# A hybrid decoder step: two sigmoids and one PSUM read of the second LRU group moved ahead in their engines' programs

## The chip, the cores and the metric

One core of a Trainium2 chip runs the whole kernel. The metric is the device time of one execution in microseconds, as the median of several runs. Engines are called by their short names in the profile: PE is TensorE's matmul, PEld its weight load, DVE is VectorE, ACT is ScalarE, POOL is GpSimd, SP is SyncE.

## The reference, cut to what matters

One inference step of a two-layer decoder over 512 prompt tokens and 8 sample tokens, 520 columns in all, in float32. Each layer adds a retention branch and an LRU branch, merged by sigmoid gates, and then a SwiGLU. The change lies in the LRU branch:

```python
def rg_lru(xc, w_a, b_a, w_x, b_x, lam, h0):
    r = sigmoid(einsum('blnc,ncd->blnd', xb, w_a) + b_a)
    i = sigmoid(einsum('blnc,ncd->blnd', xb, w_x) + b_x)
    log_a = -LRU_C * r * softplus(-lam)
    a = exp(log_a)
    u = sqrt(-expm1(2.0 * log_a)) * (i * xf)
    _, h = associative_scan(comb, (a, u), axis=1)
xc, new_buf = causal_conv(x_lru, conv_buf, conv_w, conv_b)
hl, h_last = rg_lru(xc, ...)
lru_branch = (gelu(y_lru) * hl) @ w_lru_out
```

The convolution has four taps. The LRU's width is 1280, that is ten tiles of 128 channels.

## The kernel before

Activations lie transposed, channels on the 128 partitions and the 520 tokens along them, in two halves of 260. Every product in float32 is made of three matmuls of split operands (high by high, low by high, high by low), so each operand is kept as a high part and a low part. The weights come as a stream: SP loads a unit of up to eight 128x128 blocks into one of two buffers, POOL writes its high part (L356, a scaling copy) and its low part (L358, a subtraction) in two halves, four blocks and the rest, and PE multiplies (`product`, L370). POOL may overwrite half a buffer once PE has gone on from it (semaphore w_used).

Each engine has its own program, written out in order, and the engines meet by semaphores alone. An engine that waits holds up all that stands behind it in its program.

In the LRU stage the ten tiles are two groups of five, (g, t). A tile goes through these steps:

- PE makes the projected x. DVE reads it (`read_x`, L1115). ACT applies the first tap with the bias (`first_tap`, L1537 to L1539), DVE the three others (`conv`, L1123 and three times L1126), ACT writes the high part (`conv_high`, L1546), DVE the low part (`conv_low`, L1135).
- PE makes three results for (g, t): the two gates from the convolved x, and the projected y (`gates`). ACT reads the two gates through the sigmoid (`gate_sigmoids`, L1557 and L1560); DVE reads y (`read_y`, L1162).
- ACT goes on with two exponentials, tanh, gelu and a square root (`gate_decay`, L1566 to L1574). DVE multiplies the second gate (`gate_input`, L1169), forms a factor once tanh is there (`one_less_a2`, L1175), scans (`scan`, L1182 to L1189), and both write the split result (`gated_high`, L1551 and L1552; `gated_low`, L1194).
- In group 1, PE puts between the tiles the output products of group 0 (`lru_out`), which DVE reads (`read_out`, L1201).

PE's results of the stage go through a ring of four PSUM slots, and result n can start only when result n-4 has been read (`ring_begin`, `freed`). The results around the change are these positions of the ring's count:

- 23, 24, 25: first gate, second gate and y of (1,0), read by the two sigmoids and by read_y(1,0)
- 26, 27: output products 0 and 1 of group 0, read by read_out(0) and read_out(1)
- 28, 29, 30: the gates and y of (1,1)
- 31: output product 2; 32, 33, 34: the gates and y of (1,2)

A gate of (1,0) has two blocks, of (1,1) three; a y has eight, an output product five. So 27 waits for the read of 23, 28 for that of 24, 29 for that of 25, 30 for that of 26, and 34 for that of 30, read_y(1,1).

PE makes in this part, in order: gates(0,4), x of (1,2), x of (1,3), x of (1,4), gates(1,0), output products 0 and 1, gates(1,1), and so on. PE's program is the same before and after.

The table of ScalarE's functions is loaded by an instruction of its own (ACT_TABLE_LOAD, put in ahead of the first function that needs another table).

Of the kernel before, what the change touches and what calls it, by code (L numbers as in the profile page):

```python
# [133 lines left out]
def build(nc, wstream, xt, params, norms, tables, dec, kdt, slru, sconv, sret, ident,  # L134
          yt, ret_p, ret_s, lru_o, conv_p, conv_s, vscr):
    ctx = ExitStack()
    with ctx:
# [131 lines left out]
        def halves(ap):  # L269

            return ap.rearrange("p (t b) -> p t b", t=2)
# [6 lines left out]
        def ring(n):  # L278

            return PP[:, n % RING, :, 0:HALF] if n % RING < 2 else (  # L280
                AUX[:, 2 * (n % RING) - 4:2 * (n % RING) - 2, 0:HALF])
# [495 lines left out]
        def _(dve):  # L777
# [40 lines left out]
            with dve.Fori(0, DEPTH) as layer:  # L818
# [284 lines left out]
                def r_done(n, more=0):  # L1103
                    dve.wait_ge(s["r_done"], layer * R_TILES + (n + 1) + more)
# [13 lines left out]
                def conv(g, t):  # L1118

                    c = g * GT + t  # L1120
                    xr = XR[:, c % 2, :]
                    dve.wait_ge(s["tap_full"], layer * LT + (c + 1))
                    tt(XCF[:, t, SEQ:TOK], XCF[:, t, SEQ:TOK], SCS[:, c, :], ALU.add)  # L1123
                    for j in range(CW - 1):
                        d = CW - 1 - j
                        m = stt(XCF[:, t, d:SEQ], xr[:, 0:SEQ - d], CUR[:, PC_CW + c * CW + j:PC_CW + c * CW + j + 1],  # L1126
                                XCF[:, t, d:SEQ], ALU.mult, ALU.add)
                        if j < CW - 2:
                            dve.drain()  # L1129
                    m.then_inc(s["xc_full"], 1)  # L1130

                def conv_low(g, t):
                    dve.drain()
                    dve.wait_ge(s["xc_high"], layer * LT + (g * GT + t + 1))
                    tt(XCL[:, t, :], XCF[:, t, :], XCH[:, t, :].bitcast(F32), ALU.subtract  # L1135
                       ).then_inc(s["xc_low"], 1)
# [21 lines left out]
                def read_y(g, t):  # L1158
                    n = LRU_TILE["y", g, t] + 2
                    dve.drain()  # L1160
                    r_done(n)
                    tt(halves(YF[:, t % 2, :]), ring(n), halves(RINV[:]), ALU.mult  # L1162
                       ).then_inc(r_free[n % RING], 1)

                def gate_input(g, t):

                    b, n = t % 2, LRU_TILE["y", g, t]
                    dve.wait_ge(*freed(layer, n + 1))
                    tt(IX[:, b, :], IX[:, b, :], XCF[:, t, :], ALU.mult)  # L1169

                def one_less_a2(g, t):

                    b, c = t % 2, g * GT + t
                    dve.wait_ge(s["th_full"], layer * LT + (c + 1))
                    stt(DF[:, b, :], DF[:, b, :], 1.0, LA[:, b, :], ALU.add, ALU.mult).then_inc(s["d_full"], 1)  # L1175

                def scan(g, t):

                    b, c = t % 2, g * GT + t
                    tt(HF[:, SEQ:TOK], AF[:, b, SEQ:TOK], SLR[:, c, :], ALU.mult)  # L1180
                    dve.wait_ge(s["w_sqrt"], layer * LT + (c + 1))
                    tt(IX[:, b, :], IX[:, b, :], DF[:, b, :], ALU.mult)  # L1182
                    dve.drain()
                    dve.tensor_tensor_scan(HF[:, 0:SEQ], AF[:, b, 0:SEQ], IX[:, b, 0:SEQ], 0.0,  # L1184
                                           ALU.mult, ALU.add)
                    tt(HF[:, SEQ:TOK], HF[:, SEQ:TOK], IX[:, b, SEQ:TOK], ALU.add)
                    dve.drain()  # L1187
                    dve.wait_ge(s["y_gelu"], layer * LT + (c + 1))
                    tt(YF[:, b, :], YF[:, b, :], HF, ALU.mult).then_inc(s["gl_full"], 1)  # L1189

                def gated_low(g, t):
                    dve.drain()
                    dve.wait_ge(s["gl_high"], layer * LT + (g * GT + t + 1))
                    tt(GL[g][1][:, t, :], YF[:, t % 2, :], GL[g][0][:, t, :].bitcast(F32), ALU.subtract  # L1194
                       ).then_inc(s["gl_low"], 1)

                def read_out(m_):

                    n = LRU_TILE["o", 0, m_]
                    r_done(n)  # L1200
                    ts(halves(ACCL[:, m_, :]), ring(n), 1.0, None, ALU.mult).then_inc(r_free[n % RING], 1)  # L1201
# [16 lines left out]
                    gated_low(0, t)  # L1218
                conv_low(*FILL_X[GT - 1])
                conv(1, 3)  # L1220
                conv_low(1, 3)
                conv(1, 4)
                for t in range(GT):
                    if t == 0:
                        conv_low(1, 4)
                    else:
                        gated_low(1, t - 1)
                    gate_input(1, t)
                    read_y(1, t)
                    one_less_a2(1, t)  # L1230
                    for m_ in FILL_O[t]:
                        read_out(m_)
                    scan(1, t)
# [93 lines left out]
        def _(act):  # L1327
# [45 lines left out]
            with act.Fori(0, DEPTH) as layer:  # L1373
# [155 lines left out]
                def r_done(n, more=0):  # L1529
                    act.wait_ge(s["r_done"], layer * R_TILES + (n + 1) + more)  # L1530

                def first_tap(g, t):

                    c = g * GT + t
                    xr = XR[:, c % 2, :]
                    act.wait_ge(s["xr_full"], layer * LT + (c + 1))
                    A(CVP[:, c, :], xr[:, SEQ - CW + 1:SEQ], copy)  # L1537
                    A(CVS[:, c, CW - 2, :], xr[:, SEQ:TOK], copy)
                    A(XCF[:, t, :], xr, ACT.Identity, bias=CUR[:, PC_CB + c:PC_CB + c + 1],  # L1539
                      scale=CUR[:, PC_CW + c * CW + CW - 1:PC_CW + c * CW + CW]).then_inc(s["tap_full"], 1)  # L1540

                def conv_high(g, t):
                    if g:
                        r_done(LRU_TILE["y", 0, min(t + 1, GT - 1)] + 1)
                    act.wait_ge(s["xc_full"], layer * LT + (g * GT + t + 1))
                    A(XCH[:, t, :], XCF[:, t, :], copy).then_inc(s["xc_high"], 1)  # L1546

                def gated_high(g, t):
                    c = g * GT + t
                    act.wait_ge(s["gl_full"], layer * LT + (c + 1))  # L1550
                    A(LRO[:, c, :], HF[:, SEQ - 1:TOK], copy)  # L1551
                    A(GL[g][0][:, t, :], YF[:, t % 2, :], copy).then_inc(s["gl_high"], 1)  # L1552

                def gate_sigmoids(g, t):
                    b, c, n = t % 2, g * GT + t, LRU_TILE["y", g, t]
                    r_done(n)
                    A(halves(LA[:, b, :]), ring(n), ACT.Sigmoid,  # L1557
                      bias=CUR[:, PC_BA + c:PC_BA + c + 1]).then_inc(r_free[(n) % RING], 1)
                    r_done(n + 1)
                    A(halves(IX[:, b, :]), ring(n + 1), ACT.Sigmoid,  # L1560
                      bias=CUR[:, PC_BX + c:PC_BX + c + 1]).then_inc(r_free[(n + 1) % RING], 1)

                def gate_decay(g, t):
                    b, c, n = t % 2, g * GT + t, LRU_TILE["y", g, t]
                    act.drain()
                    A(AF[:, b, :], LA[:, b, :], ACT.Exp, scale=LAM[:, 4, c:c + 1])  # L1566
                    A(DF[:, b, :], LA[:, b, :], ACT.Exp, scale=LAM[:, 5, c:c + 1])
                    act.drain()
                    A(LA[:, b, :], LA[:, b, :], ACT.Tanh, scale=CUR[:, PC_SP + c:PC_SP + c + 1]
                      ).then_inc(s["th_full"], 1)  # L1570
                    act.wait_ge(*freed(layer, n + 2))
                    A(YF[:, b, :], YF[:, b, :], ACT.Gelu_apprx_tanh).then_inc(s["y_gelu"], 1)
                    act.wait_ge(s["d_full"], layer * LT + (c + 1))
                    A(DF[:, b, :], DF[:, b, :], ACT.Sqrt).then_inc(s["w_sqrt"], 1)  # L1574
# [6 lines left out]
                for t in range(GT):  # L1581
                    gate_sigmoids(0, t)
                    conv_high(*((0, 2) if t == 0 else FILL_X[t - 1]))
                    gate_decay(0, t)
                    first_tap(*FILL_X[t])
                    gated_high(0, t)
                conv_high(*FILL_X[GT - 1])
                first_tap(1, 3)
                conv_high(1, 3)
                first_tap(1, 4)  # L1590
                for t in range(GT):
                    gate_sigmoids(1, t)
                    if t == 0:
                        conv_high(1, 4)
                    else:
                        gated_high(1, t - 1)
                    gate_decay(1, t)
# [253 lines left out]
```

## Time and profile before

| what | us |
|---|---|
| median of 3 runs | 2459.19 |
| lowest and highest run | 2458.72, 2462.03 |
| the profiled execution's own time | 2456.01 |
| its span in the profile | 2454.2 |

The profile is of one execution. Its PE clock was granted at 0.998 of full speed on average. Times within it are microseconds from the start of the span. Layer 0's LRU stage lies from about 510 to 690, layer 1's 1211.9 later with the same pattern. In a timeline row the first number is the start and the second the duration; what stands in brackets at its end is the idle time before it, and what ended that. The recorded durations of neighbouring matmuls overlap, since they are pipelined.

### The profile page before, as it was taken

The page shows a single profiled execution, that of the slowest core. Times are in us where ns is not written, and L with a number is a line of the kernel's source. Part 1 is how long each engine was busy: PE and PEld are TensorE (multiplying, and loading weights), DVE is VectorE, ACT ScalarE, POOL GpSimd, SP SyncE. Part 2 cuts the span into 40 slices and gives each one's busy share as a digit, 9 for nine tenths or more (in the row PEclk, how much of TensorE's full clock was granted, in tenths as well). Part 3 has the DMA queues.
Part 4 walks back from the last instruction along what each step waited for, and adds up shares of the span by engine and source line. Part 5 has one row for each costly group of instructions (what it writes and reads, how often), then busy time and mean ns, then how long its engine had stood idle before and what let it go on. Part 6 is the DMA issues. An engine that isn't in the chain of part 4 may idle for free.

```text
span 2454.2 us, 53114 instructions
## 1 busy us (share of the span) xinstructions
PE 2423.3 (99%) x19640; PEld 2364.6 (96%) x19640; DVE 1178.2 (48%) x1587; ACT 645.1 (26%) x982; POOL 1634.4 (67%) x1685
## 2 busy tenths in 40 slices
PE   8999999999999999999999999999999999999998
PEld 7999999999999999999999999999999999999998
DVE  8646363678644432022266373736786454211223
ACT  2404040446811211011114041413666112100111
POOL 6464646578887776776765555555888776667765
PEclk9999999999999999999999999999999999999999
DMA  5636363522232222322257373645223232223222
GB/s 209 237 121 244 121 241 117 206 87 91 85 102 92 95 90 81 104 90 83 94 166 250 114 250 120 239 133 190 88 91 90 97 95 91 90 82 103 91 85 88
DMA packets 121737, 315.51 MB, mean 129 GB/s; under 512 B 12192, under 2 KB 12960, under 8 KB 121568
## 3 DMA queue, kind: packets, MB, share of 16 engines
q1 hardware_dynamic: 60480, 199.78, 25.5%
q10 hardware_dynamic: 61088, 113.34, 13.0%
q8 instruction: 123, 2.02, 0.3%
q14 instruction: 46, 0.38, 0.0%
HBM read 272.69 MB, written 40.38 MB: 128 GB/s over the span
## 4 chain that ended last, share of the span: by engine, by line
PE 91%; DVE 4%; DVEq 2%; ACT 1%; issue 1%; DMA 0%; ACTq 0%
PE proj L370 55%; PE aux L370 27%; PE aux L625 2%; DVE scratch L1126 2%; PE aux L582 1%; PE aux L555 1%; PE proj L633 1%; PE aux L633 1%; DVEq L1129 1%; DVE scratch L1184 1%; PE aux L611 1%; PE proj L625 0%; DVEq L807 0%; DVEq L1160 0%; DVEq L1187 0%
## 5 line engine op out<-in xcount | busy, mean ns | idle before, releaser
L358 POOL TENSOR_TENSOR w_low<-w_raw,w_high 128x512 fp32r<-128x512 f32 x840 | 1091.1, 1299 | 124.5 <-issue 2.1
L356 POOL TENSOR_SCALAR w_high<-w_raw 128x512 fp32r<-128x512 f32 x840 | 549.7, 654 | 674.1 <-PE proj L370 495.4
L370 PE MATMUL proj<-x_high,w_high 128*128 128x260 f32 x2752 | 558.8, 284 | 11.4 <-DVE x_low L797 11.0
L370 PE MATMUL proj<-x_high,w_low 128*128 128x260 f32 x2752 | 555.0, 283 | 0.0
L370 PE MATMUL proj<-x_low,w_high 128*128 128x260 f32 x2752 | 554.1, 283 | 0.0
L370 PEld LDWEIGHTS proj<-x_high,w_high 128*128 128x128 f32 x2752 | 425.3, 189 | 20.6 <-issue 16.9
L370 PEld LDWEIGHTS proj<-x_high,w_low 128*128 128x128 f32 x2752 | 424.8, 189 | 0.0
L370 PEld LDWEIGHTS proj<-x_low,w_high 128*128 128x128 f32 x2752 | 424.0, 189 | 0.0
L370 PE MATMUL proj<-split_scratch,w_high 128*128 128x260 f32 x2544 | 409.2, 283 | 0.0
L370 PEld LDWEIGHTS proj<-split_scratch,w_high 128*128 128x128 f32 x2544 | 348.6, 188 | 5.0 <-issue 5.0
L370 PE MATMUL aux<-x_high,w_high 128*128 128x260 f32 x1344 | 270.9, 283 | 0.0
L370 PE MATMUL aux<-x_high,w_low 128*128 128x260 f32 x1344 | 270.7, 283 | 0.0
L370 PE MATMUL aux<-x_low,w_high 128*128 128x260 f32 x1344 | 270.2, 283 | 0.0
L370 PE MATMUL proj<-split_scratch,w_low 128*128 128x260 f32 x1272 | 255.9, 282 | 0.0
L370 PE MATMUL aux<-split_scratch,w_high 128*128 128x260 f32 x1456 | 233.7, 282 | 5.6 <-ACT scratch L1557 5.6
L370 PEld LDWEIGHTS aux<-x_high,w_high 128*128 128x128 f32 x1344 | 207.2, 188 | 0.1
L370 PEld LDWEIGHTS aux<-x_high,w_low 128*128 128x128 f32 x1344 | 207.1, 188 | 0.0
L370 PEld LDWEIGHTS aux<-x_low,w_high 128*128 128x128 f32 x1344 | 206.7, 188 | 0.0
L370 PEld LDWEIGHTS aux<-split_scratch,w_high 128*128 128x128 f32 x1456 | 199.4, 188 | 6.0 <-POOL w_low L358 6.0
L370 PEld LDWEIGHTS proj<-split_scratch,w_low 128*128 128x128 f32 x1272 | 196.0, 188 | 0.0
L370 PE MATMUL aux<-split_scratch,w_low 128*128 128x260 f32 x728 | 146.4, 282 | 0.0
L370 PEld LDWEIGHTS aux<-split_scratch,w_low 128*128 128x128 f32 x728 | 112.2, 188 | 0.0
(197 smaller groups left out, 2283.5 us busy)
## 6 DMA issues: line engine op xcount, KB each, us to landing
w_raw<-in_wstream SPq DMA_DIRECT2D x252, 512.0 KB, 3.5
scratch<-in_sret ACTq DMA_DIRECT2D x96, 512.0 KB, 6.9
out_ret_s<-scratch ACTq DMA_DIRECT2D x64, 512.0 KB, 4.4
w_raw<-in_wstream SPq DMA_DIRECT2D x72, 448.0 KB, 3.3
w_raw<-in_wstream SPq DMA_DIRECT2D x48, 384.0 KB, 3.0
scratch<-v_rows ACTq DMA_DIRECT2D x64, 256.0 KB, 3.9
w_raw<-in_wstream SPq DMA_DIRECT2D x48, 320.0 KB, 2.9
out_ret_p<-scratch ACTq DMA_DIRECT2D x8, 512.0 KB, 5.5
```

The lines of the kernel that those rows point to most:

```text
L356: pool.tensor_scalar(WH[:, j, w], WR[:, j, w], 1.0, 0.0, ALU.mult, ALU.add)
L358: pool.tensor_tensor(WL[:, j, w], WR[:, j, w], WH[:, j, w].bitcast(F32), ALU.subtract).then_inc(s["w_split"], 1)
L370: m = pe.matmul(out, wt[:, w, blk * P:(blk + 1) * P], x[xi], start=first and n == 0, stop=last and n == 2)
L555: m = pe.matmul(AUX[QUAD * r:QUAD * (r + 1), BANK["RO"], :], QZ[:, d, SRING * n + r, :], SS[r][:, d, :], start=n == d == 0, stop=n == NBAT ...
L582: m = pe.matmul(aux(f"SC{j}")[:, 0:SEQ - j * P], a[:, d, j * P:(j + 1) * P], b[:, d, j * P:SEQ], start=d == n == 0, stop=d == KT - 1 and n ...
L611: m = pe.transpose(aux(f"TV{j}")[:, e * P:(e + 1) * P], VF[:, e, j * P:(j + 1) * P], ID[:])
L625: m = pe.matmul(aux(f"AT{t}"), a[:, w], b[:, j, :], start=j == n == 0, stop=j == t and n == 2)
L633: m = pe.matmul(aux(f"ST{d}"), a[:, j, d * P:(d + 1) * P], b[:, j, :], start=j == n == 0, stop=j == TT - 1 and n == 2)
L1126: m = stt(XCF[:, t, d:SEQ], xr[:, 0:SEQ - d], CUR[:, PC_CW + c * CW + j:PC_CW + c * CW + j + 1], XCF[:, t, d:SEQ], ALU.mult, ALU.add)
L1129: dve.drain()
L1184: dve.tensor_tensor_scan(HF[:, 0:SEQ], AF[:, b, 0:SEQ], IX[:, b, 0:SEQ], 0.0, ALU.mult, ALU.add)
```

## The change

On ScalarE the two sigmoids of tile (1,0) go ahead of conv_high(1,2), first_tap(1,3), conv_high(1,3) and first_tap(1,4). On VectorE read_y(1,0) goes from behind gate_input(1,0) to behind conv(1,3), ahead of conv_low(1,3) and conv(1,4).

```diff
@@ VectorE @@
                 conv_low(*FILL_X[GT - 1])
                 conv(1, 3)
+                read_y(1, 0)
                 conv_low(1, 3)
                 conv(1, 4)
                 for t in range(GT):
@@ VectorE @@
                     gate_input(1, t)
-                    read_y(1, t)
+                    if t:
+                        read_y(1, t)
                     one_less_a2(1, t)
@@ ScalarE @@
                     gated_high(0, t)
+                gate_sigmoids(1, 0)
                 conv_high(*FILL_X[GT - 1])
                 first_tap(1, 3)
                 conv_high(1, 3)
                 first_tap(1, 4)
                 for t in range(GT):
-                    gate_sigmoids(1, t)
+                    if t:
+                        gate_sigmoids(1, t)
```

ScalarE before, from the end of first_tap(1,3) to the first sigmoids of group 1 and conv_high(1,4):

```order
L1539 ACTIVATE scratch<-scratch,params_cur 128x520
L1546 ACTIVATE split_scratch<-scratch 128x520
L1536 REGISTER_ALU
L1537 ACTIVATE conv_p_sb<-scratch 128x3
L1538 ACTIVATE conv_s_sb<-scratch 128x8
L1539 ACTIVATE scratch<-scratch,params_cur 128x520
L1530 REGISTER_ALU
L1557 ACT_TABLE_LOAD
L1557 ACTIVATE scratch<-aux,params_cur 128x520
L1530 REGISTER_ALU
L1560 ACTIVATE scratch<-proj,params_cur 128x520
L1546 ACTIVATE split_scratch<-scratch 128x520
```

ScalarE in the changed kernel, from the end of gated_high(0,4) to conv_high(1,3) (its lines are numbered two higher: L1557 is now L1559, L1546 is L1548):

```order
L1554 ACTIVATE split_scratch<-scratch 128x520
L1532 REGISTER_ALU
L1559 ACT_TABLE_LOAD
L1559 ACTIVATE scratch<-aux,params_cur 128x520
L1532 REGISTER_ALU
L1562 ACTIVATE scratch<-proj,params_cur 128x520
L1548 ACTIVATE split_scratch<-scratch 128x520
L1538 REGISTER_ALU
L1539 ACTIVATE conv_p_sb<-scratch 128x3
L1540 ACTIVATE conv_s_sb<-scratch 128x8
L1541 ACTIVATE scratch<-scratch,params_cur 128x520
L1548 ACTIVATE split_scratch<-scratch 128x520
```

The table load and the two sigmoids stand right behind gated_high(0,4), with two high parts and two first taps behind them that stood ahead. The number of rows and of table loads of ScalarE's program is the same in both kernels.

VectorE at the same place, between the last two taps of conv(1,3) and conv_low(1,3), as a piece of the difference:

```order
 L1126 SCALAR_TENSOR_TENSOR scratch<-scratch,params_cur 128x510
 L1126 SCALAR_TENSOR_TENSOR scratch<-scratch,params_cur 128x511
+L1104 REGISTER_ALU
+L1162 TENSOR_TENSOR scratch<-proj,rinv 128x520
 L1135 TENSOR_TENSOR split_scratch<-scratch,split_scratch 128x520
 L1122 REGISTER_ALU
```

The read of y has come in ahead of conv_low(1,3). It is gone between gate_input (L1169) and one_less_a2 (L1175). POOL's and SP's programs are the same in both kernels.

## Rows read from the trace of the kernel before

**Rows 1.** The page: busy time, share of the span, instructions, per engine.

```profile
PE 2423.3 (99%) x19640; PEld 2364.6 (96%) x19640; DVE 1178.2 (48%) x1587; ACT 645.1 (26%) x982; POOL 1634.4 (67%) x1685
```

**Rows 2.** Waits of PE over the span: us in total, times, longest.

```profile
PE proj L370 <- DVE x_low L797: 11.0, 4, 8.0
PE aux L370 <- ACT scratch L1557: 5.6, 2, 2.8
```

**Rows 3.** Timeline of PE in layer 0: start, duration, instruction.

```profile
614.47 0.71 PE L370 MATMUL aux<-split_scratch,w_high 128*128 128x260 f32 x4 [2.80 <-ACT scratch L1557]
...
620.29 0.64 PE L370 MATMUL proj<-split_scratch,w_high 128*128 128x260 f32 x4
...
622.46 0.40 PE L370 MATMUL aux<-x_high,w_high 128*128 128x260 f32 x2
...
636.13 0.40 PE L370 MATMUL aux<-x_high,w_high 128*128 128x260 f32 x2
```

**Rows 4.** Timeline of ACT in layer 0.

```profile
600.86 0.62 ACT L1552 ACTIVATE split_scratch<-scratch 128x520 fp32r<-128x520 f32 x1
604.28 0.64 ACT L1546 ACTIVATE split_scratch<-scratch 128x520 fp32r<-128x520 f32 x1 [2.80 <-DVE scratch L1126]
...
612.34 1.28 ACT L1557 ACT_TABLE_LOAD   x1
613.63 0.69 ACT L1557 ACTIVATE scratch<-aux,params_cur 128x520 f32<-128x520 f32 x1
614.23 0.69 ACT L1560 ACTIVATE scratch<-proj,params_cur 128x520 f32<-128x520 f32 x1
616.18 0.64 ACT L1546 ACTIVATE split_scratch<-scratch 128x520 fp32r<-128x520 f32 x1 [1.26 <-DVE scratch L1126]
...
619.60 0.73 ACT L1569 ACTIVATE scratch<-scratch,params_cur 128x520 f32<-128x520 f32 x1
```

**Rows 5.** Timeline of DVE in layer 0.

```profile
606.99 3.69 DVE L1126 SCALAR_TENSOR_TENSOR scratch<-scratch,params_cur 128x509 f32<-128x509 f32 x3
611.45 1.06 DVE L1135 TENSOR_TENSOR split_scratch<-scratch,split_scratch 128x520 fp32r<-128x520 f32 x1 [0.77 <-ACT split_scratch L1546]
...
613.58 2.50 DVE L1126 SCALAR_TENSOR_TENSOR scratch<-scratch,params_cur 128x509 f32<-128x509 f32 x3
...
618.31 0.70 DVE L1162 TENSOR_TENSOR scratch<-proj,rinv 128x520 f32<-128x520 f32 x1 [0.15 <-PE aux L370]
620.36 0.75 DVE L1175 SCALAR_TENSOR_TENSOR scratch<-scratch 128x520 f32<-128x520 f32 x1 [1.35 <-ACT scratch L1569]
621.03 1.29 DVE L1201 TENSOR_SCALAR scratch<-aux 128x520 f32<-128x520 f32 x2
...
630.75 0.70 DVE L1162 TENSOR_TENSOR scratch<-aux,rinv 128x520 f32<-128x520 f32 x1 [0.15 <-issue]
```

**Rows 6.** The chain that ended last, two taps of conv(1,3) in it.

```profile
607.07 1.10 DVE scratch L1126
...
608.24 1.62 DVE scratch L1126
```

**Rows 7.** Timeline of POOL in layer 0.

```profile
607.02 0.62 POOL L356 TENSOR_SCALAR w_high<-w_raw 128x512 fp32r<-128x512 f32 x1
607.78 1.53 POOL L358 TENSOR_TENSOR w_low<-w_raw,w_high 128x512 fp32r<-128x512 f32 x1
...
611.35 0.62 POOL L356 TENSOR_SCALAR w_high<-w_raw 128x512 fp32r<-128x512 f32 x1 [0.34 <-PE aux L370]
612.12 1.52 POOL L358 TENSOR_TENSOR w_low<-w_raw,w_high 128x512 fp32r<-128x512 f32 x1
615.03 0.52 POOL L356 TENSOR_SCALAR w_high<-w_raw 128x384 fp32r<-128x384 f32 x1 [1.40 <-PE aux L370]
...
617.94 0.70 POOL L356 TENSOR_SCALAR w_high<-w_raw 128x512 fp32r<-128x512 f32 x1 [0.99 <-PE aux L370]
618.79 1.29 POOL L358 TENSOR_TENSOR w_low<-w_raw,w_high 128x512 fp32r<-128x512 f32 x1
```

## The prediction

> **What bounds the kernel now.** I read the page's engine shares first: PE is busy for 2423.3 of 2454.2 us, every other engine far less [rows 1]. So only what makes PE wait can change the time. The waits of PE come next: in the stage of the change there is one kind, 5.6 us in all, twice 2.8 us, once per layer, and it names ScalarE's L1557, the first sigmoid of a group [rows 2]. The larger wait on L797 (11.0 us) lies elsewhere and isn't touched.
>
> PE's timeline places it (layer 0; layer 1 repeats it with the same 2.8 us, so every figure below counts twice). The ring positions are those of the section on the kernel before. PE stands idle for 2.80 us before position 27, which starts at 614.47 and could have started at 611.7 [rows 3]. It needs position 23, the sums of the first gate of group 1, to have been read. ScalarE reads it at 613.63, behind a table load at 612.34 [rows 4], because its program has two high parts and two first taps ahead. Those wait for VectorE's taps. ScalarE stands idle 2.80 us before the high part at 604.28: time in which the sigmoids could run. The wait of both layers, 5.6 us or 0.23%, is the most that the change can give.
>
> **The change on ScalarE.** Nothing is added: one table load and two sigmoids move, past conv_high(1,2), first_tap(1,3), conv_high(1,3) and first_tap(1,4). The last instruction now ahead is the high part at 600.86 that lasts 0.62 [rows 4]. It ends at 601.5; then 1.28 for the load, 0.6 to the second sigmoid's start (613.63 to 614.23) and 0.69 for it put the end at 604.1. PE has made positions 23 and 24 by then: it has 25 (eight blocks) and 26 (five) still to do before 611.7 at 0.72 us a block (position 29's three blocks take 620.29 to 622.46), so 24 ended near 602.3. conv_high(1,2) starts at 604.28 in the trace, so it isn't delayed: 0 us, hidden in the idle 2.80 us, with 0.2 us to spare. The taps and high parts find the sigmoid's table loaded instead of the square root's. In the order of the changed program they bring no load of their own, so the count of loads stays. After first_tap(1,4) ScalarE is now free from 612.3 and waits for VectorE's last taps: conv_high(1,4) still can't start before they end (616.18 in the trace), and the chain of exponentials and tanh behind it is as late as before. No DMA is issued by what moves. Position 27 is free at 603.5 and position 28 (needs 24) at 604.1.
>
> A table load is followed directly by its sigmoid here: 612.34 plus 1.28 is 613.62, and the sigmoid starts at 613.63 [rows 4]. The Trainium skill, page "ScalarE: Activation LUTs", section "What ACT_TABLE_LOAD costs", adds a drain of about 1.38 us to the load, 2.66 us for a switch. By that the sigmoids would end near 605.5 and the sum would be that of rival (d). The trace disagrees (no such gap), and I take the trace.
>
> **The change on VectorE.** Without the second part position 29, which needs 25, would be late: PE would want it at 620.29 - 2.8 = 617.5, and read_y(1,0) runs at 618.31 to 619.0 [rows 3, 5]. Moved up, it starts behind the third tap of conv(1,3), at about 610.9. VectorE has 0.77 us of idle time there before conv_low(1,3) at 611.45, because it waits for ScalarE's high part [rows 5]. The read takes 0.70 us; its PSUM operand has long been made, and it shows the same 0.70 when a POOL instruction is in flight (618.31 against POOL's 617.94 to 618.64 [rows 5, 7]). So conv_low(1,3) is asked for at 611.75 instead of 611.45. In the trace it lasts 1.06 instead of 0.70, because POOL's scaling copy is at work until 611.97 [rows 7]; it would end at 612.5 either way. The move costs 0 us and may cost up to 0.3.
>
> **What is late next.** PE would now want position 30 at 622.46 - 2.8 = 619.7. It needs position 26 read, which is read_out(0) on VectorE: 621.03, the first half of a pair of 1.29, so it ends near 621.7 [rows 3, 5]. In VectorE's order it stands behind one_less_a2(1,0), at 620.36, which waits for the tanh of 619.60 [rows 4, 5], at the end of the chain from conv(1,4). Nothing in the change makes that chain earlier. PE answers a release within 0.14 us (a sigmoid ending 614.33, PE at 614.47). If VectorE keeps its times, position 30 starts at 621.85 instead of 622.46: of 2.8 us saved only **0.6 us per layer** survives, and a new wait of 2.2 us takes the place of the old.
>
> Does VectorE keep its times? Two-input SBUF work on VectorE and POOL exclude each other in this trace. The tap at 607.07 lasts 1.10 and the one at 608.24 lasts 1.62 (ends 609.86), against POOL's 607.02 to 607.64 and 607.78 to 609.31: each ends some 0.53 us after POOL's instruction [rows 6, 7]. Conv(1,3) as a whole takes 3.69 us, conv(1,4) at 613.58 only 2.50, because POOL was idle from 613.64 to 615.03, waiting 1.40 us for the stalled PE [rows 5, 7]. That gap goes with the stall: POOL may start its next copy at 613.6. I play the same alternation as in conv(1,3): POOL 0.52, first tap ends 614.65; POOL's subtraction of 0.97 (three quarters of the 1.29 at 618.79, for three blocks instead of four) until 615.5, second tap 616.05; the next copy of 0.62, third tap 617.05. Against 616.08 before, **conv(1,4) ends 1.0 us later** (bounds: 0 where POOL leaves the gaps, 3.69 - 2.50 = 1.2 us as in conv(1,3)). I take 1.0: the rows of conv(1,3) are the nearest, same shapes and same neighbour.
>
> ScalarE's chain follows by 1.0, so tanh ends at 621.3. one_less_a2 then meets POOL at its next unit: between 0 and 1.29 us more (the subtraction at 618.79 [rows 7]). In the trace it slips in behind POOL's copy at no cost, and I take 0 for the forecast. Then read_out(0) ends at 622.7 and position 30 starts at about 622.8: **0.3 us later than before, per layer**.
>
> **Behind it.** PE's lead or lag is carried to the end where nobody waits: the next reads have room. Position 34 needs read_y(1,1), 630.75 to 631.45, and PE gets there at 636.13, 4.7 us later [rows 3, 5]. A chain later by 1 to 2 us is absorbed. Sum: 2 x 0.3 = +0.6 us. Against the profiled execution's own 2456.01 us that makes 2456.6; it lies 3.2 us under the median of the runs shown (2459.19), so the forecast as a median is 2459.19 + 0.6 = **2459.8 us**.
>
> **Rivals.**
> (a) VectorE keeps its times: 0.6 us saved per layer, 2458.0. For it: POOL has slack and may yield at each tap. Against: the pattern of conv(1,3). Chance 0.34.
> (b) The full 2.8 us per layer comes through, 2453.6. It needs read_out(0) done by 619.5, before its own predecessor's tanh has been computed. Only if conv(1,4) were to end over 2 us sooner. Chance 0.03.
> (c) Slower: all the POOL work brought forward is put ahead of VectorE's chain. That is 0.52 + 0.97 + 0.62 + 1.29 = 3.4 us on a release of 621.85, so position 30 at 625.25, 2.8 us late per layer, 2464.8. It decides from 2.5 us per layer on. Smaller doses, one_less_a2 losing one 1.29 us turn, give 1.6 us per layer and 2462.4. Chance of the small dose 0.15, of the full one 0.03.
> (d) ScalarE's block doesn't fit before 604.28, because the switch to the sigmoid takes as long again as its load, 1.28 us more [rows 4]. With 0.2 us to spare conv_high(1,2) and all behind it shift by up to 1.1 us on top of the forecast, 1.4 us per layer, 2462.0. Against: the moved sigmoid follows its load at once in rows 4. Chance 0.02. The Trainium skill's page "ScalarE: Activation LUTs", section "What ACT_TABLE_LOAD costs", would give the switch that time.
> My forecast has the rest, 0.43.
>
> **How the numbers follow.** The range takes in (a), the forecast and the small dose of (c), 2458.0 to 2462.4, and below it 1.5 us because the three runs and the profiled one scatter by as much: 2456.5 to 2462.5. A measurement of this kernel can tell from no change about 0.2%, 4.9 us. Faster by more than that is (b), 0.03; slower by more is (c)'s full dose, 0.03; the rest, 0.94, is within.
>
> **What would show it.** In the profile after: PE's wait on L1557 (now L1559) gone, sigmoids at 602.8 to 604.1, read_y(1,0) at 610.9, conv_high(1,2) still at 604.28. In its place a PE wait of 2 to 4 us on VectorE's read of position 26 (L1201) in each layer. POOL without its 1.40 us gap at 613.6, and conv(1,4) at 3.5 us or so instead of 2.50. The forecast is wrong if PE has no new wait, or if conv(1,4) keeps 2.50 us and PE is 0.6 us ahead at position 30, or if conv_high(1,2) is late.

## The result, and the profile after

The changed kernel takes 2464.7 us (median of 8 runs, 2461.33 to 2465.73), the kernel before 2458.88 beside it (8 runs, 2454.38 to 2462.52). The ratio is 1.0021, with a 95% interval of 1.0012 to 1.0031: slower by about 0.2%, some 5 to 6 us. The forecast was no change to speak of, 2459.8, in a range up to 2462.5; the result lies 2.2 us above that range.

The page and PE's waits after, as [rows 1, 2] of before:

```profile
PE 2427.7 (99%) x19640; PEld 2368.6 (96%) x19640; DVE 1176.4 (48%) x1587; ACT 645.6 (26%) x982; POOL 1633.8 (66%) x1685
```

```profile
PE proj L370 <- DVE x_low L797: 11.2, 4, 8.2
PE aux L370 <- DVE scratch L1201: 8.5, 2, 4.2
```

The wait of twice 2.8 us on the sigmoid is gone, and one of twice 4.2 us on read_out has come. PE is also busy for 4.4 us more, though its instructions are the same ones. The next rows say where 3.2 of them come from; the other 1.2 come at the end of the span and are told below. PE's timeline in layer 0, as [rows 3]:

```profile
621.36 0.40 PE L370 MATMUL proj<-split_scratch,w_low 128*128 128x260 f32 x2
625.99 0.51 PE L370 MATMUL aux<-x_high,w_high 128*128 128x260 f32 x2 [4.23 <-DVE scratch L1201]
...
628.46 0.64 PE L370 MATMUL aux<-x_high,w_high 128*128 128x260 f32 x2
...
633.37 0.64 PE L370 MATMUL aux<-split_scratch,w_high 128*128 128x260 f32 x4
```

The same place by stretches of 2 us (columns: stretch and its length; busy time and number of instructions of PE, PEld, DVE, ACT, POOL; granted clock; DMA share; GB/s):

```profile
626.00:628.00 2.00, 2.00 (x10) 2.00 (x11) 1.15 (x3) 1.97 (x3) 0.22 (x1) 0.59 0.00 0
628.00:630.00 2.00, 2.00 (x12) 2.00 (x11) 1.85 (x4) 1.99 (x3) 1.56 (x2) 0.56 0.00 0
630.00:632.00 2.00, 2.00 (x19) 2.00 (x18) 1.20 (x3) 1.42 (x4) 0.28 (x1) 1.00 0.56 147
```

Position 30 is at 625.99. In this execution everything in layer 0 up to there is 2.17 us later than in the profile of before (the taps of conv(1,3) start at 609.16 against 606.99), a difference that arose at the start and has nothing to do with the change. Less 2.17 it is 623.82, against 622.46 before: **1.36 us later**. Position 31 is at 633.37, less 2.17 is 631.20, against 628.23: **2.97 us later**. The 1.61 us between the two come from PE itself: for about 3.5 us after the wait the granted clock is near half (1.2 GHz in place of 2.4), and pairs of matmuls follow each other every 0.43 us instead of 0.24. Layer 1, with its own offset of 5.01, gives 1.35 and 2.96. Twice 2.97 is 5.9 us, and the medians differ by 5.8. That these two agree so closely is in part luck, since the profile of before is of a fast execution (2456.01, where the median beside the change is 2458.88).

The profiled execution of the changed kernel took 2465.30 us, 9.3 more than that of before. Besides the 5.9 us of this stage, 2.2 arose in the first 50 us of the span, and 1.2 among the last matmuls, where the granted clock is lower sooner. Here is the changed kernel, then the kernel before (it is some 8 us ahead there, so nearly the same place in the program):

```profile
2450.00:2455.00 5.00, 4.42 (x21) 4.33 (x21) 0.19 (x1) 0.88 (x2) 0.00 (x0) 0.50 0.00 0
```

```profile
2441.00:2446.00 5.00, 4.23 (x24) 4.05 (x24) 1.08 (x3) 1.57 (x3) 0.00 (x0) 0.65 0.00 0
```

Experiments 3 and 4 show the same 1.2 us at the end, the other profiles don't, so it isn't put down to the change. Together with twice 1.61 us it makes up the 4.4 us that PE is busy longer.

DVE, ACT and POOL in layer 0, as [rows 4, 5, 7]:

```profile
609.16 3.70 DVE L1126 SCALAR_TENSOR_TENSOR scratch<-scratch,params_cur 128x509 f32<-128x509 f32 x3
613.03 0.70 DVE L1162 TENSOR_TENSOR scratch<-proj,rinv 128x520 f32<-128x520 f32 x1 [0.17 <-issue]
613.82 0.87 DVE L1135 TENSOR_TENSOR split_scratch<-scratch,split_scratch 128x520 fp32r<-128x520 f32 x1
...
615.78 3.50 DVE L1126 SCALAR_TENSOR_TENSOR scratch<-scratch,params_cur 128x509 f32<-128x509 f32 x3
...
623.56 1.76 DVE L1175 SCALAR_TENSOR_TENSOR scratch<-scratch 128x520 f32<-128x520 f32 x1 [1.64 <-ACT scratch L1571]
625.25 1.29 DVE L1201 TENSOR_SCALAR scratch<-aux 128x520 f32<-128x520 f32 x2
```

```profile
604.96 0.70 ACT L1559 ACTIVATE scratch<-aux,params_cur 128x520 f32<-128x520 f32 x1
605.56 0.69 ACT L1562 ACTIVATE scratch<-proj,params_cur 128x520 f32<-128x520 f32 x1
606.45 0.64 ACT L1548 ACTIVATE split_scratch<-scratch 128x520 fp32r<-128x520 f32 x1 [0.21 <-DVE scratch L1126]
...
619.38 0.64 ACT L1548 ACTIVATE split_scratch<-scratch 128x520 fp32r<-128x520 f32 x1 [4.88 <-DVE scratch L1126]
...
622.80 0.73 ACT L1571 ACTIVATE scratch<-scratch,params_cur 128x520 f32<-128x520 f32 x1
```

```profile
614.29 1.55 POOL L358 TENSOR_TENSOR w_low<-w_raw,w_high 128x512 fp32r<-128x512 f32 x1
615.81 0.51 POOL L356 TENSOR_SCALAR w_high<-w_raw 128x384 fp32r<-128x384 f32 x1
...
623.50 1.26 POOL L358 TENSOR_TENSOR w_low<-w_raw,w_high 128x512 fp32r<-128x512 f32 x1
```

The moved pieces do what they should: the sigmoids fit with 0.21 us to spare, conv_high(1,2) at 606.45 is 604.28 plus the offset, and the early read of y costs conv_low(1,3) nothing. Then POOL's gap of 1.40 us is gone (615.81 follows at once), conv(1,4) takes 3.50 us instead of 2.50, the tanh comes 1.03 us later, and one_less_a2 meets POOL's subtraction of 623.50 and takes 1.76 us instead of 0.75. Read_out(0) stands behind it, and PE behind that.

The forecast agreed up to the tanh. Open were: is read_out's place really what bounds PE now, does POOL's work cause the longer taps, what does each half of the change do alone, and when does PE's clock fall.

### The profile page after: what moved, and what is told of

Same layout as the page of the kernel before. It is cut to its first block, busy times and chain, and to the rows that moved or that the text cites. A ratio compares the mean times of both kernels' runs of the same rounds, so it can differ in the third digit from the quotient of the medians.

```text
span 2463.4 us, 53114 instructions
## 1 busy us (share of the span) xinstructions
PE 2427.7 (99%) x19640; PEld 2368.6 (96%) x19640; DVE 1176.4 (48%) x1587; ACT 645.6 (26%) x982; POOL 1633.8 (66%) x1685
## 4 chain that ended last, share of the span: by engine, by line
PE 90%; DVE 4%; ACT 2%; DVEq 2%; issue 1%; ACTq 0%; DMA 0%
PE proj L370 55%; PE aux L370 27%; DVE scratch L1126 2%; PE aux L625 2%; PE aux L582 1%; PE aux L555 1%; PE proj L633 1%; PE aux L633 1%; DVEq L1129 1%; DVE scratch L1184 1%; PE aux L611 1%; ACT L1568 0%; PE proj L625 0%; DVEq L1187 0%; ACT L1574 0%
```

## The experiments

Each kernel was timed beside the kernel before on the same chip. Beside experiments 1 to 4 the kernel before had 2459.24 us (30 runs, 2456.69 to 2462.92), beside 5 to 8 it had 2459.1 (25 runs, 2456.18 to 2461.66).

### 1. The read of position 26 out of the chain

To the change is added:

```diff
                 conv(1, 4)
+                read_out(0)
                 for t in range(GT):
...
                     for m_ in FILL_O[t]:
-                        read_out(m_)
+                        if m_:
+                            read_out(m_)
```

> The change with read_out(0), the read of position 26, moved from behind one_less_a2(1,0) to right behind conv(1,4), into VectorE's wait for ScalarE's high part. Theory (the wait went over from position 27 to position 30, whose release stood behind the tanh; POOL's earlier work made it later still; PE's clock fell after the longer wait): PE waits for nothing between positions 23 and 31 or under 0.5 us in each layer, no stretch at the lower clock there, so about 2 x 2.8 = 5.6 us under the kernel before, some 2453.3 against 2458.9, and 11 us under the change. Conv(1,4) keeps its 3.5 us. Rival 1 (a chain of VectorE and ScalarE bounds the stage, so the read's place is of no account): PE waits as long at position 31 or 32, no gain. Rival 2 (the change costs through ScalarE's moved table load): the time stays at the change's.

Measured: 2452.87 us (8 runs, 2451.81 to 2454.5), ratio to the kernel before 0.9974 (0.9964 to 0.9985). That is 6.4 us under before, 11.8 under the change. Of PE's waits in the stage this is left:

```profile
PE aux L370 <- DVE scratch L1162: 1.1, 2, 0.7
```

DVE and PE in layer 0 (this execution is 1.57 us late against before at the taps of conv(1,3)):

```profile
615.11 3.50 DVE L1126 SCALAR_TENSOR_TENSOR scratch<-scratch,params_cur 128x509 f32<-128x509 f32 x3
618.54 0.69 DVE L1201 TENSOR_SCALAR scratch<-aux 128x520 f32<-128x520 f32 x1
...
622.89 1.81 DVE L1175 SCALAR_TENSOR_TENSOR scratch<-scratch 128x520 f32<-128x520 f32 x1 [1.65 <-ACT scratch L1573]
```

```profile
635.21 0.51 PE L370 MATMUL aux<-x_high,w_high 128*128 128x260 f32 x2 [0.45 <-DVE scratch L1162]
```

```profile
634.46 0.70 DVE L1162 TENSOR_TENSOR scratch<-aux,rinv 128x520 f32<-128x520 f32 x1 [0.15 <-issue]
```

The taps still take 3.50 us and one_less_a2 1.81: VectorE's chain is as late as in the change. It no longer matters to PE, since the read sits ahead of it in a wait of VectorE's own. Rival 1, that the chain bounds the stage wherever the read stands, falls: what is left of it is the 0.45 and 0.67 us at position 34, for read_y(1,1). That read had 4.7 us to spare before. Now PE comes 2.8 us sooner, and VectorE reads 2.1 us later (634.46 less 1.57 is 632.89, against 630.75), which uses it up. Rival 2, that the moved table load costs, falls as well: the load is where the change has it, and the time isn't the change's.

The waits in the stage have gone from 5.6 to 1.1 us, which is 4.5 us, and the two profiles agree with that: PE leaves the stage 2.3 and 2.1 us sooner in the two layers. The medians differ by 6.4. Experiments 3, 6 and 7 show what the other 1.9 us are likely to be: a lower clock that the kernel before has in some executions.

### 2. ScalarE's half alone

```diff
                 conv(1, 3)
-                read_y(1, 0)
                 conv_low(1, 3)
...
-                    if t:
-                        read_y(1, t)
+                    read_y(1, t)
```

> ScalarE's half of the change alone, read_y(1,0) back at its old place. Theory: PE waits in two parts, some 2.7 us at position 29 (for read_y, itself 1.0 us later because conv(1,4) again takes 3.5 us beside POOL) and 0.4 to 1.4 us at position 30. If the clock falls only after the long single wait, position 31 starts about 1.4 us later than before per layer and the whole is +2.7 us, 2461.6 where the kernel before has 2458.9. Rival 1 (the moved read on VectorE is what costs): conv(1,4) at 2.50 us and no loss against before. Rival 2 (the clock falls after any loss of this sum): +5.8 us as in the change.

Measured: 2462.14 us (10 runs, 2456.49 to 2463.12), ratio 1.0009 (1.0 to 1.0019), so the interval just touches no change. The number was as expected, the way there only in part:

```profile
621.33 1.24 PE L370 MATMUL proj<-split_scratch,w_high 128*128 128x260 f32 x4 [3.21 <-DVE scratch L1162]
```

```profile
622.00:624.00 2.00, 2.00 (x11) 2.00 (x11) 1.92 (x4) 1.97 (x3) 0.51 (x1) 0.50 0.60 203
```

There is one wait, 3.21 us at position 29, and none at 30: the clock is at its lower level behind the wait in both layers of this profile, and a PE at half speed comes to position 30 after read_out has been done. I had expected the lower clock only behind the longer wait of the change. The profiled execution took 2462.92, near the top of its runs. The three runs with a mean clock of 0.995 average 2462.9 us, the six with 0.996 2460.7, so it probably didn't fall for as long, or in both layers, in all of them; only one of them has a trace, so this isn't shown.

### 3. VectorE's half alone

```diff
                 conv(1, 3)
+                read_y(1, 0)
                 conv_low(1, 3)
                 conv(1, 4)
                 for t in range(GT):
...
-                    read_y(1, t)
+                    if t:
+                        read_y(1, t)
```

> VectorE's half of the change alone, the sigmoids at their old place. Theory: PE's wait at position 27 on ScalarE's sigmoid stays at 2.8 us per layer, POOL's idle gap stays, conv(1,4) keeps about 2.50 us, position 30 starts as before: 0 us, within 1 us of the kernel before. Rival (the moved read delays the chain to the tanh by itself): conv(1,4) or one_less_a2 0.5 us or more later, PE waits at position 30 too, and the time is 1 us or more over the kernel before.

Measured: 2459.61 us (10 runs, 2456.41 to 2462.4), ratio 0.9999 (0.999 to 1.0008). The wait at position 27 stays, and so do POOL's gap and the short taps:

```profile
PE aux L370 <- ACT scratch L1559: 5.6, 2, 2.8
```

```profile
614.95 2.50 DVE L1126 SCALAR_TENSOR_TENSOR scratch<-scratch,params_cur 128x509 f32<-128x509 f32 x3
```

The early read costs nothing by itself. Layer 1 of this profile had a surprise: the same wait, and behind it the lower clock, which neither layer of the first profile of before had shown. PE's row and the stretch behind it:

```profile
1827.33 1.20 PE L370 MATMUL aux<-split_scratch,w_high 128*128 128x260 f32 x4 [2.81 <-ACT scratch L1559]
```

```profile
1828.00:1830.00 2.00, 2.00 (x11) 2.00 (x11) 1.17 (x2) 0.70 (x2) 1.77 (x2) 0.50 0.00 0
```

### 4. POOL held back

POOL waits for the end of the last convolution of the layer before it writes the second half of the first weight unit of tile (1,1), the piece ahead of which it stood idle for 1.40 us in the kernel before:

```diff
                                 pool.wait_ge(s["w_used"], u + (h + 2))
+                                if base + k == LRU_UNIT["y", 1, 1] and h == 1:
+                                    pool.wait_ge(s["xc_full"], layer * LT + LT)
```

> The change, and POOL waits for the end of conv(1,4) before it writes the second half of the first weight unit of tile (1,1), so that its idle gap is back though PE isn't stalled. Theory (POOL's work brought forward makes the taps and the tanh chain 1.0 us late): conv(1,4) back at 2.5 us, tanh 1.0 us sooner, PE's wait at position 30 between 2.2 and 3.2 us instead of 4.2; if it is under some 3 us the clock stays up as it did after the 2.8 us of before. Then position 31 starts 0.6 us earlier to 0.5 us later than before per layer, 2457.7 to 2459.9. Rival 1 (the taps are long for another reason): conv(1,4) stays at 3.5 us. Rival 2 (POOL's hold only makes the weights late): PE waits for w_low at position 29 or 30 and the time stays above 2462.

Measured: 2458.35 us (10 runs, 2455.73 to 2459.87), ratio 0.9995 (0.9986 to 1.0005), 6 us under the change. DVE, POOL and PE in layer 0 (1.30 us late against before; lines are numbered two higher):

```profile
614.84 2.38 DVE L1128 SCALAR_TENSOR_TENSOR scratch<-scratch,params_cur 128x509 f32<-128x509 f32 x3
...
621.50 1.07 DVE L1177 SCALAR_TENSOR_TENSOR scratch<-scratch 128x520 f32<-128x520 f32 x1 [1.39 <-ACT scratch L1573]
```

```profile
617.42 0.51 POOL L358 TENSOR_SCALAR w_high<-w_raw 128x384 fp32r<-128x384 f32 x1 [2.52 <-DVE scratch L1128]
```

```profile
619.61 0.75 PE L372 MATMUL proj<-split_scratch,w_high 128*128 128x260 f32 x4 [0.24 <-POOL w_low L360]
623.24 0.51 PE L372 MATMUL aux<-x_high,w_high 128*128 128x260 f32 x2 [1.93 <-DVE scratch L1203]
```

With POOL out of the way the taps take 2.38 us. It is POOL that makes them long. Position 30 starts at 623.24, less 1.30 is 621.94: this is rival (a) of the prediction, which had 621.85. The wait there is 1.93 us, a little shorter than I expected because the weights cost PE 0.24 us ahead of it, and the clock stays up in both layers. Rival 2, late weights, is there with these 0.24 us and no more.

### 5. A longer wait in the kernel before

```diff
+                A(TOUCH, EPST, ACT.Exp)
                 for t in range(GT):
                     gate_sigmoids(1, t)
```

> The kernel before, with one more table load on ScalarE (an exponential of one column, whose result nobody reads) ahead of gate_sigmoids(1,0): PE's wait at position 27 grows from 2.8 to about 4.3 us per layer, and nothing else moves. Theory (a wait of 4 us is followed by some 3.5 to 6 us in which the granted clock is at 1.2 GHz instead of 2.4, in every execution, a wait of 2.8 us only in some): +3.0 us of waiting, and +1.6 to +3 us per layer of lower clock where it wasn't there yet, 2464 to 2467 against 2459.2, and both layers of the profile show the lower clock. Rival (the clock fell in the changed kernel because of what ran around the wait, not because of its length): +3.0 us alone, 2462.2, and full clock in both layers.

Measured: 2463.96 us (10 runs, 2461.97 to 2465.63), ratio 1.0021 (1.0011 to 1.0031). This is just under the expected 2464. The wait is 4.30 and 4.32 us, and the granted clock in stretches behind it is at its lower level in both layers (0.52 at 618 to 620, 0.50 at 1832 to 1834). PE in both layers and the stretch behind it:

```profile
616.81 1.21 PE L370 MATMUL aux<-split_scratch,w_high 128*128 128x260 f32 x4 [4.30 <-ACT scratch L1557]
1830.86 0.71 PE L370 MATMUL aux<-split_scratch,w_high 128*128 128x260 f32 x4 [4.32 <-ACT scratch L1557]
```

```profile
618.00:620.00 2.00, 2.00 (x12) 2.00 (x11) 2.00 (x2) 1.99 (x3) 1.35 (x2) 0.52 0.00 0
1832.00:1834.00 2.00, 2.00 (x11) 2.00 (x10) 1.99 (x2) 1.99 (x3) 1.35 (x1) 0.50 0.00 0
```

The rival, full clock in both layers, falls. The wait alone accounts for 3.0 of the 4.9 us. The rest, 1.9 us, is less than the 1.6 to 3 us per layer of the expectation. That fits a kernel before that has some of it already (experiment 7); how much isn't measured here.

### 6. The early read_out without the change

```diff
                 conv(1, 4)
+                read_out(0)
                 for t in range(GT):
...
-                        read_out(m_)
+                        if m_:
+                            read_out(m_)
```

> The kernel before with read_out(0) right behind conv(1,4) and nothing else moved. Theory (position 30's release has 0.6 us to spare as long as PE waits at position 27): 0 us, within 1 us of 2459.2, PE's wait of 2.8 us stays at position 27. Rival (the early read is good by itself, by shortening the chain behind it): 1 us or more faster.

Measured: 2459.21 us (10 runs), ratio 1.0006 (0.9996 to 1.0015). No effect, as expected: the wait of 2.8 us stays at position 27. The 6.4 us of experiment 1 belong to the combination.

### 7. The kernel before once more

> The kernel before, profiled once more. Theory (the wait of 2.8 us is followed by a lower clock in some executions and not in others): the two layers may differ from the first profile; a layer whose position 27 runs at the lower clock ends it 1.5 to 3 us later. If both layers show the full clock, this profile says nothing for or against.

Measured: one execution, 2458.16 us. PE in layer 0 and the stretch behind:

```profile
615.16 0.82 PE L370 MATMUL aux<-split_scratch,w_high 128*128 128x260 f32 x4 [2.80 <-ACT scratch L1557]
```

```profile
617.00:619.00 2.00, 2.00 (x11) 2.00 (x10) 1.32 (x3) 1.92 (x3) 0.63 (x1) 0.50 0.10 8
```

Layer 0 has the lower clock, layer 1 has not. Position 28 comes at 620.37, 5.21 us behind the start of position 27; in the first profile it is 3.68 us (618.15 less 614.47), so the lower clock cost 1.5 us. So the kernel before itself loses some time in this way in part of its executions. Its 30 runs agree: the 4 with a mean clock of 0.998 average 2457.3 us, the 15 with 0.997 average 2459.0, the 9 with 0.996 2459.7, the 2 with 0.995 2462.5. The first profile, of a run of 2456.01 us, was one of those without it.

### 8. The early read_out without the early read of y

The edits are those of experiments 1 and 2 together: sigmoids early, read_out(0) early, read_y(1,0) late.

> The version with read_out(0) moved early, but read_y(1,0) at its old place. Theory (each of the three reads bounds PE in its turn): PE waits about 3.2 us at position 29 for read_y(1,0), as in the run of ScalarE's half alone, with the lower clock behind it, so about that run's time, 2461 to 2463, and no gain from the early read_out. Rival (read_y's place doesn't matter once read_out is early): 2453 to 2456.

Measured: 2461.65 us (10 runs, 2459.13 to 2463.6), ratio 1.0012 (1.0002 to 1.0021), as experiment 2. PE waits 3.21 us at position 29:

```profile
621.35 1.21 PE L370 MATMUL proj<-split_scratch,w_high 128*128 128x260 f32 x4 [3.21 <-DVE scratch L1162]
```

The rival falls. Each read bounds PE in its turn, and of the versions run only the one with all three moved frees it. The two reads of VectorE moved without the sigmoids were not run; experiments 3 and 6, where each is moved alone, keep the wait on the sigmoid.

## Why the prediction was wrong

Right, by its steps: what bounds PE (the waits name it), ScalarE's block fits into the idle time (0.2 us to spare was expected, 0.21 measured), no second table cost (rival (d) falls: conv_high(1,2) is on time), the early read costs nothing, the new wait lies at position 30 behind read_out(0), POOL's gap goes and conv(1,4) ends 1.0 us later (1.0 measured, and experiment 4 shows POOL as its cause).

Two terms went wrong, one in size and one left out. The first is in "What is late next": one_less_a2 meets POOL, "between 0 and 1.29 us more", and "I take 0 for the forecast". It took 1.76 us instead of 0.75, 1.0 us more, and as much in layer 1 and in experiment 1 (1.81). I had its rival, the small dose of (c), at 0.15 with 1.6 us per layer; measured is 1.36 at position 30. My own timeline had both engines ask at about the same moment, and the row I leaned on, the cheap 0.75 of before, was taken with POOL at another point of its cycle. (The forecast's own terms give position 30 at 621.85 + 0.97 = 622.82, 0.36 us late, where its sum has 0.3; with the 1.0 us of one_less_a2 that is the 1.36 measured.) Position 30 alone gives 2 x 1.36 = 2.7 us, 2461.9, still within the range.

The step that failed is in "Behind it": "PE's lead or lag is carried to the end" was taken at full clock. The sum priced the new wait, 4.2 us where the old one was 2.8, by its difference alone, and put what PE does after a wait at nothing, without a reason. In the profile it ran 1.6 us longer over position 30 in each layer. Experiment 5 shows that the change's edits aren't needed for it: a wait of 4.3 us in the kernel before is followed by the same, at the same total of 1.0021. The 1.6 us are no fixed price, though. In the eleven layers that have the lower clock, what PE loses in the stage beyond its waits is 1.4 to 2.8 us (1.5 in experiment 7, 2.7 in layer 1 of experiment 3). The kernel before pays something of this kind too, in some executions (experiment 7, and experiments 3 and 6 behind the same 2.8 us). So against a typical execution of before the loss by these two terms should be smaller than against the profile that I had.

Experiment 1 allows a check of the sum, since PE hardly waits there and keeps its clock. From its 2452.87 us, the change's longer waits (8.5 us in place of 1.1) and twice 1.6 us of clock give an estimate of 2463.4. Measured is 2464.7, so 1.3 us stay open. Four of the change's eight runs have a mean clock of 0.994 or 0.995, below the 0.996 of the profiled one, so the price may be higher in them. That isn't shown, since only one execution of each kernel has a trace, and two of the kernel before.

Over all ten profiles, each with two layers, this is how waits in this stage and the lower clock went together: 0.7 us or less, 0 of 2; 1.93 us, 0 of 2; 2.80 to 2.82 us, 3 of 8 (before, before again, experiments 3 and 6); 3.21 us, 4 of 4; 4.2 to 4.3 us, 4 of 4.

The rival that was nearest in the number is the full dose of (c), 2464.8, with a chance of 0.03. It hit by luck. It had position 30 2.8 us late per layer from POOL's work alone; measured is 1.36, and the clock behind it makes up the 2.97. The small dose, 2462.4, had the mechanism of the delay nearly in full (one_less_a2 behind one turn of POOL) and nothing of the clock.

## What to carry to other kernels

When a wait is removed from a bounding engine, list the next few releases in order with their spare time, and ask of each what stands ahead of it in its own engine's program: here three reads bounded PE one behind the other, two of them moved and the kernel got slower, and the third move, 0.7 us of work put where VectorE stood idle, made it faster than before (ratio 0.9974). A wait of PE can cost more than its length, since the clock may fall behind it (here by 1.4 to 2.8 us). And a stall also gives other engines room, here VectorE beside a POOL that had nothing to do; that room goes with it.

## What the runs showed of the hardware that I had not expected

In a stage that is otherwise full, the granted clock was at half behind every single wait of PE of 3.2 to 4.3 us (8 of 8 layers), and stayed there for some 3 to 6 us of matmuls. At the 2.8 us of the kernel before it fell in 3 of 8 layers, with the same program of PE on either side. This probably makes up part of the 6 us by which executions of one kernel differ: where PE hardly waits (experiment 1) the 8 runs lie within 2.7 us. Other parts are at the start of the span, where the profiles differ by up to 2.2 us, and among its last matmuls, with 1.2 us in 3 of 10 profiles.
